# Earlier sums of the activations and one more up unit as seven half-block products in a fused two-block kernel

## The reference

```
x  = x + g1 * (concat(y_hy, y_gla) @ w_out)
h2 = rms_norm(x, norm_mlp) * (1 + sc2) + sh2
x  = x + g2 * (square(relu(h2 @ w1)) @ w2)      # w1: 1024 x 4096, w2: 4096 x 1024
return rms_norm(x, norm_final)
```

## Time and profile before

| | |
|---|---|
| median of 3 runs | 1623.96 us (1623.46 to 1624.85) |
| the profiled execution | 1624.14 us |
| its span | 1622.3 us |
| PE busy | 99% of the span |
| DVE, ACT, POOL busy | 59%, 45%, 35% |
| share of PE in the chain that ended last | 91% |
| share of DVE in it | 6% |

### The profile page before, as it was taken

One profiled execution on the slowest core, in us unless ns is written; L12 is line 12 of the kernel. 1 busy time (PEld: TensorE's weight loads), 2 busy tenths in 40 slices (PEclk: granted clock), 3 DMA queues, 4 the chain that ended last, 5 costly groups with the idle time before them and its releaser, 6 DMA issues.

```text
span 1622.3 us, 21503 instructions
## 1 busy us (share of the span) xinstructions
PE 1599.2 (99%) x8740; PEld 1350.2 (83%) x8740; DVE 959.7 (59%) x1435; ACT 735.7 (45%) x1107; POOL 571.6 (35%) x289
## 2 busy tenths in 40 slices
PE   9999999999999999999999999999999989999998
PEld 6888898888888878888887767789878769999997
DVE  7788867676666364443443646681356785555554
ACT  7533343443432433555455464423535645555554
POOL 1002113221344434334333334353323215555552
PEclk9999999999999999999999999999999999999999
DMA  6454334343455323233223241122112223233321
GB/s 241 153 198 131 131 123 135 115 132 120 133 206 207 104 91 105 93 103 99 97 91 122 78 156 65 53 82 78 45 48 69 74 91 103 94 103 104 104 91 53
DMA packets 53259, 179.25 MB, mean 110 GB/s; under 512 B 6428, under 2 KB 7068, under 8 KB 52776
## 3 DMA queue, kind: packets, MB, share of 16 engines
q1 hardware_dynamic: 53160, 177.88, 32.8%
HBM read 172.58 MB, written 2.12 MB: 108 GB/s over the span
## 4 chain that ended last, share of the span: by engine, by line
PE 91%; DVE 6%; ACT 2%; issue 1%; DMA 0%; POOL 0%; SPq 0%; DVEq 0%; ACTq 0%; POOLq 0%
PE banks L450 89%; PE banks L453 2%; DVE wl L1224 1%; DVE ACC L1260 1%; DVE X L1193 1%; ACT T L2095 0%; DVE ada L1193 0%; DVE XSL L2017 0%; DVE XW L1999 0%; DVE T L1990 0%; ACT wh L2098 0%; ACT XSH L2098 0%; DMA raw<-wst_dram 0%; ACT Sc L2095 0%; ACT FHI L2098 0%
## 5 line engine op out<-in xcount | busy, mean ns | idle before, releaser
L2698 POOL TENSOR_TENSOR wl<-raw,wh 128x1024 fp32r<-128x1024 f32 x139 | 345.6, 2491 | 425.0 <-ACT wh L2098 425.0
L450 PE MATMUL banks<-HH,wh 128*128 128x512 f32 (+2 forms) x944 | 363.9, 388 | 7.7 <-DVE X L1193 6.0
L450 PE MATMUL banks<-HL,wh 128*128 128x512 f32 (+2 forms) x944 | 353.5, 380 | 0.4 <-DVE HL L1193 0.4
L2098 ACT ACTIVATE wh<-raw 128x1024 fp32r<-128x1024 f32 x246 | 256.6, 1050 | 206.9 <-PE banks L450 194.6
L450 PE MATMUL banks<-HH,wl 128*128 128x512 f32 (+1 forms) x936 | 251.0, 380 | 0.0
L450 PEld LDWEIGHTS banks<-HH,wh 128*128 128x128 f32 (+1 forms) x944 | 177.7, 188 | 47.6 <-issue 11.9
L450 PEld LDWEIGHTS banks<-HL,wh 128*128 128x128 f32 (+1 forms) x944 | 177.6, 188 | 35.7 <-issue 1.4
L450 PEld LDWEIGHTS banks<-HH,wl 128*128 128x128 f32 x936 | 172.8, 189 | 33.8 <-issue 1.0
L450 PE MATMUL banks<-wh,HH 128*128 128x256 f32 x448 | 128.5, 287 | 0.0
L450 PE MATMUL banks<-wl,HH 128*128 128x256 f32 x448 | 126.7, 283 | 0.0
L450 PE MATMUL banks<-wh,HL 128*128 128x256 f32 x448 | 126.6, 283 | 0.0
(11 more groups left out here) (392 smaller groups left out, 3150.2 us busy)
## 6 DMA issues: line engine op xcount, KB each, us to landing
raw<-wst_dram SPq DMA_DIRECT2D x294, 512.0 KB, 3.4
X<-xT_dram SPq DMA_DIRECT2D x8, 512.0 KB, 5.8
CB<-sums_dram SPq DMA_DIRECT2D x12, 256.0 KB, 3.1
D<-dec_dram SPq DMA_DIRECT2D x12, 256.0 KB, 2.8
out_dram<-XT SPq DMA_DIRECT2D x8, 256.0 KB
QS<-QX SPq DMA_DIRECT2D x24, 64.0 KB, 2.9
KSw<-KX SPq DMA_DIRECT2D x24, 64.0 KB, 2.0
MX<-memT_dram SPq DMA_DIRECT2D x2, 512.0 KB, 9.0
```

The costliest lines, as they stand in the source:

```text
L450: return pe.eng.matmul(dst, w, x, start=start, stop=stop, skip_group_check=True)
L2098: return eng.activation(dst, src, ACT.Copy)
L2698: tt(wl[:, q, :], raw[:, i % NRAW, :], wh[:, q, :].bitcast(F32), ALU.subtract).then_inc(*by_pool("low", u))
```

## The change

`SEVEN` goes from 4 to 3, so unit 3 is made as seven products as well: its tiles 190 and 191 get block sums. Tiles 190 and 191 are listed no more in DVE_LOW (their low part is made by DVE in the other branch of `split`). Unit 2 is written to banks 4 and 5 in place of 0 and 1. The sums of the activations move forward in the lists of DVE and ACT: x_sums(0) and x_whole(1) stand ahead of unit 2's squares, x_sums_low(0) behind them, x_sums(1) behind down(0,0), x_sums_low(1) behind down(0,1). On ACT, x_sums_high(0) stands ahead of unit 2's relu and x_sums_high(1) behind the split that comes with down(0,0). GpSimd makes the FLO of all hidden tiles from the seventh on.

```diff
--- before.py
+++ after.py
@@ -46,7 +46,7 @@
 
 
 
-SEVEN = 4
+SEVEN = 3
 
 
 def weight_plan():
@@ -123,7 +123,7 @@
 S_AT = {u: v for v, u in enumerate(S_TILES)}
 NS = 3
 
-DVE_LOW = frozenset([*range(73), 164, *range(186, 194)])
+DVE_LOW = frozenset([*range(73), 164, 186, 187, 188, 189, 192, 193])
 
 
 def ada_targets(g):
@@ -1148,7 +1148,7 @@
             if u >= SEVEN:
                 seven(u)
             else:
-                unit_f(("up", u), (2, 3) if u == 1 else (0, 1), *hi_lo("x4"), by_k=2 if u == 1 else 0)
+                unit_f(("up", u), (2, 3) if u == 1 else (4, 5), *hi_lo("x4"), by_k=2 if u == 1 else 0)
 
         def down(g, n):
             u = feed.take()
@@ -2042,18 +2042,21 @@
                 seven(u)
                 return
             g = u // 2
+            if u == 2:
+                x_sums(0)
+                x_whole(1)
             for j in range(2):
                 k = 2 * (u % 2) + j
                 t = turn("hidden", g, k)
                 square(g, k, t)
                 if made[0] % 3 == 0:
                     temp_used("hidden", g, k)
+            if u == 2:
+                x_sums_low(0)
             if u == 1:
                 for j in range(2):
                     square(g, j, E[j])
                 x_whole(0)
-            if u > 1:
-                x_sums(u - 2)
 
         def down(g, n):
             for j in range(2):
@@ -2071,10 +2074,10 @@
                 stt(X[:, t, :], bank[DOWN_BANKS[n % 2][j]], mod[:, 40 + t:41 + t], X[:, t, :], ALU.mult, ALU.add).then_inc(*by_dve("kept", ("down", g, n), j))
                 if g == 7:
                     add_square("x5", t, T, t == 0, t == 6, free=done("sum", "x3"))
-            if g == 0 and n in (0, 2):
-                x_sums_low(n // 2)
+            if (g, n) == (0, 0):
+                x_sums(1)
             if (g, n) == (0, 1):
-                x_whole(1)
+                x_sums_low(1)
 
         for step in FF[1:]:
             (up if step[0] == "up" else down)(*step[1:])
@@ -2639,18 +2642,18 @@
                 for k in (2 * (u % 2) + 1, 2 * (u % 2)):
                     high(g, k, temp("hidden", g, k))
                 return
+            if u == 2:
+                x_sums_high(0)
             for j in range(2):
                 k = 2 * (u % 2) + j
                 t = temp("hidden", g, k)
                 act.wait_ge(done("unit", ("up", u), j), temp_free("hidden", g, k))
-                fn(t[:, :], bank[j + 2 * (u == 1)], ACT.Relu).then_inc(*by_act("relu", g, k))
+                fn(t[:, :], bank[j + (2 if u == 1 else 4)], ACT.Relu).then_inc(*by_act("relu", g, k))
                 by_act.also("kept", ("up", u), j)
                 high(g, k, t)
             if u == 1:
                 for j in range(2):
                     high(g, j, E[j])
-            if u > 1:
-                x_sums_high(u - 2)
 
         def down(g, n):
             if (g, n) == (7, 0):
@@ -2670,6 +2673,8 @@
                 if g == 7:
                     act.wait_ge(m, done("seven", 15, 1, 3))
                     fn(XG[:, t, :], X[:, t, :], ACT.Copy, scale=P("gfin", t)).then_inc(*by_act("weighted", t))
+            if (g, n) == (0, 0):
+                x_sums_high(1)
 
         for step in FF[1:]:
             (up if step[0] == "up" else down)(*step[1:])
@@ -2829,7 +2834,7 @@
 
         def low(g, k, t):
             made[0] += 1
-            if made[0] % 3 or g >= SEVEN // 2:
+            if made[0] % 3 or made[0] > 2 * SEVEN:
                 pool.wait_ge(done("h", "f", g, k), done("f", g, k))
                 tt(FLO[g % 2][:, k, :], t[:, :], FHI[g % 2][:, k, :].bitcast(F32), ALU.subtract).then_inc(*by_pool("l", "f", g, k))
                 return True
```

## The result

The changed kernel took 1630.42 us (median of 5 runs, 1630.14 to 1631.56), the kernel before 1624.12 us beside it (1623.46 to 1624.85). The ratio is 1.004 with an interval of 1.0026 to 1.0054: slower by 6.3 us (0.4%), against 6.3 us worked out and 1630.2 forecast.

A forecast was written before the change was run, and what follows sets the result against it. PE, busy 99% of the span, was taken as the bound, with its waits for DVE's list changeable. Added 16.5 us less 10.3 removed, plus 0.1 for clock, gave 6.3 more: 1630.2 us, range 1626.5 to 1632.5 (forecast's own 1629 to 1631.5).

The forecast's parts named there:

- The pause in down(0,0): PE's bank pause inside down(0,0), with its slower first matmuls, goes because banks 0 and 1 are free: 1.8 us saved.
- the wait ahead of unit 4: PE's pause before unit 4, for DVE's line 1193, goes: 6.2 us saved.
- its slow clock: Unit 4's first half no longer runs at the slow clock that followed the long pause: 1.5 us saved.
- 0.8 us of columns: Unit 3, made as seven products, falls from 10.88 to 10.07 us on PE: 0.8 us saved.
- First wait: Ahead of unit 3, PE stands from 1306.69 to 1319.4 for DVE's addition of down(0,1): 12.7 us added.
- POOL's hold on x_sums(1): x_sums(1), issued at 1314.16 during POOL's SL, waits for POOL's end at 1315.97 and ends at 1318.50.
- Second half: Unit 3's second half waits for XSL, done at 1328.1, so PE can go at 1328.2.
- the slow stretch behind the first pause: In unit 3's first half, the same 3.08 us at half clock as before unit 4's change: 1.5 us added.
- The second pause: Between unit 3's halves, PE stands from 1325.9 to 1328.2 for XSL: 2.3 us added, plus 0.1 for the clock.
- rival 2: Clock falls in the pause between unit 3's halves or stays low through its first half: 1631.5 to 1632.9 us; chance 0.08.
- Rival 1: POOL doesn't hold DVE up in the sums' new places: 3.4 us less, 1626.8 us; chance 0.08.
- Rival 3: Not slower: moved instructions fill DVE's idle stretches and POOL never meets it: 1623.5 or 1622.0 us; chance 0.09.

The follow-up runs named there:

- the banks alone: Kernel before with unit 2, and with it plain unit 3, in banks 4 and 5, nothing else: 1624.43 us against 1624.9, ratio 0.9997.
- filler run: Changed kernel plus 46 matmuls behind down(0,1), sums unread, keeping PE busy in its long pause: 1631.76 us against 1624.56 for the kernel before, ratio 1.0044.
- spread sums: Against the kernel before: unit 3 plain, XW by POOL, units 2 and 3 in banks 4 and 5, activation sums spread out: 1619.94 us against 1624.56, ratio 0.9972.

## Why the prediction was right

**What goes.** The pause in down(0,0), the wait ahead of unit 4, its slow clock and 0.8 us of columns are gone from the trace, 10.3 us as worked out. But the run with the banks alone shows that the first of them was worth nothing by itself; the ledger's terms hold only as a set, as the difference of two schedules that end in the same work.

**What comes.** First wait 12.7 forecast, 12.63 measured. Both steps that it was worked out from hold: DVE's pieces in their new order (x_sums(1) at 1313.78 and the addition at 1318.10, against 1314.16 and 1318.50 with the 0.4 us between the traces), and POOL's hold on x_sums(1). Second half: forecast at 1328.2, measured at 1327.98, which is 1328.4 with those 0.4 us. As a ledger, measured: 12.6 for the first wait, 2.7 for the slow clock, 1.3 for the second, 16.6 added, against 12.7 + 1.5 + 2.3 = 16.5. The sum is right though two of its terms are not.

**Where a step was off.** I took the slow stretch behind the first pause as 3.08 us, as after the 6.0 us pause; it was 5.5, 1.2 us of time more. The second pause shrank by 1.0. That the two cancel is not luck: the forecast said that this pause would swallow up to 2.3 us of such a loss. The two runs of the changed kernel and the filler run confirm it: a slow stretch of 5.5, 4.2 or 0 us moved the end of the first half, and the second half began at the same point of each trace, within 0.1 us.

That the second pause cost no clock was less sure than it looked. The row taken for it, 2.40 us at 1.00, ends where the clock fell, in the same pause of the kernel before:

```profile
1332.70:1336.40 3.70, 0.00 (x0) 0.01 (x1) 3.70 (x4) 0.42 (x1) 0.69 (x1) 0.51 0.26 101
```

PE had stopped 2.3 us earlier, which is the very length forecast for the second pause. It came out at 1.3, and the clock held. In the experiments it held through 2.26 us (ahead of unit 3 in the filler run) and fell with pauses of 2.7 us (spread sums) and 3.1 us (filler, bank), so rival 2 deserved more than its 0.08.

**Rivals.** Rival 1 (POOL doesn't hold DVE up) fell: both instructions were long, and holding SL back made them short. It priced the absence of the hold at 3.4 us; the run got 1.5 to 2, and PE stood 1.7 us for the SL that then came late. Rival 3 (no slower) fell with DVE's idle stretches still in place: 1.60 us for tile 191 and 1.9 in the squares. The Trainium skill's rule of exclusion (SBUF — State Buffer, "SBUF: two separate sides") agrees with the traces wherever two such instructions met in the stretches shown, in both directions: 0.68 us became 2.35 on DVE, 2.4 became 3.21 on POOL.

**What is left open.** Why the clock's slow stretch, counted from where PE resumed, was 5.5 us in one trace and 3.1 in another. The pause's length doesn't order it: it was 3.1 us behind pauses of 6.0 and 6.4, 4.1 behind 8.3, 2.9 behind 10.9, 3.9 behind 11.5, and 5.5 and 4.2 behind the same 12.6.

## What to carry to other kernels

When an engine waits for an instruction late in another engine's list, the price is the length of that list up to the last thing needed, not the wait that the profile names: moving the named instruction (the bank addition) gained nothing, while putting the sums behind what PE wants next, with XW on GpSimd and unit 3 plain, gained 9.5 us. How much of that is GpSimd's share no run separates; where it was tried alone it gave 1 us at most. Before one more unit is given a cheaper form, set its saving (0.8 us) against what its inputs cost the fullest engine at that place. Work put on GpSimd was free for VectorE in these traces only where VectorE read a bank; its instructions with two SBUF operands stood still meanwhile.

## What the runs showed of the hardware

The granted clock (PEclk) fell 2.3 us after PE had stopped in the kernel before, and 4.2 us after it in the changed kernel. It was at the 1.2 GHz level when PE resumed after pauses of 6.0 and 12.6 us, and stayed there for 3.1 us in the one and for 5.5 and 4.2 us in two traces of the other. It also fell 0.9 us after PE had resumed, behind pauses of 2.7 us (spread sums) and 3.1 us (filler), for 3.4 and 3.2 us. It did not fall behind pauses of 1.3, 1.4, 1.85 and 2.26 us.

A DVE instruction of two SBUF operands that was issued while a GpSimd instruction ran waited until that was through (0.68 us became 2.35 under an SL of 2.34), while one that reads a bank ran its 0.74 us beside it. Where the two took turns, both stretched (2.4 to 3.21 and 2.35 to 4.51).
